# Two network blocks in one program: stage barriers replaced by stage counters, and five small reorderings

## The reference

```python
h = rmsnorm(x, norm_g[0]);  x = x + fox_mixer(h, ...)        # attention with a forget gate, 16 heads
h = rmsnorm(x, norm_g[1]);  x = x + nsa_mixer(h, ...)        # three attention branches, 16 heads
x = rmsnorm(x, final_g)
h = _rmsnorm(x, norm_mix[0]); x = x + _hgrn2_mixer(h, ...)   # gated recurrence, 8 heads of 128
h = _rmsnorm(x, norm_ffn[0]); x = x + _conv_ffn(h, ...)
h = _rmsnorm(x, norm_mix[1]); x = x + _mla_mixer(h, ...)     # latent attention, 8 heads
h = _rmsnorm(x, norm_ffn[1]); x = x + _conv_ffn(h, ...)

def _conv_ffn(h, w_up, conv_w, conv_b, w_down):              # 1024 -> 2 x 2816 -> 1024
    u = h @ w_up                                             # y: causal taps over 3 tokens of u, plus conv_b
    gate, up = jnp.split(y, 2, axis=-1)
    return (jax.nn.silu(gate) * up) @ w_down
```

## Time and profile before

| what | value |
|---|---|
| median of 3 runs | 1015.6 us (1015.43 to 1016.73) |
| time of the profiled execution | 1011.34 us |
| its span, first to last instruction | 1009.6 us |
| mean granted TensorE clock | 0.992 |
| PE, PE weight loads, DVE, ACT, POOL busy | 97%, 91%, 76%, 55%, 7% |
| bytes moved | 153.16 MB, mean 152 GB/s |

### The profile page before, as it was taken

The page is one execution under the profiler, slowest core; times in us unless marked ns, Lnnn a source line. Parts: engine busy times, 40 slices in busy tenths (PEclk is TensorE's granted clock), DMA queues, the critical chain, the costliest instruction groups (busy, mean ns, idle before and its releaser), DMA issues. The chain is left out here.

```text
span 1009.6 us, 19673 instructions
## 1 busy us (share of the span) xinstructions
PE 978.9 (97%) x7864; PEld 919.4 (91%) x7864; DVE 763.7 (76%) x1296; ACT 552.1 (55%) x873; POOL 66.8 (7%) x54
## 2 busy tenths in 40 slices
PE   7999999999999999999999999999999998999998
PEld 5999999898788999899999999999997898999996
DVE  5765776867887768498667888788868667788886
ACT  4644555365666656553566555555675464555552
POOL 3100004000000410000030000000001420000000
PEclk9999999999999999999999999999999998999999
DMA  9644445793212556500464767575531454766661
GB/s 279 178 128 131 130 146 154 219 298 110 84 43 83 156 180 187 190 1 1 148 187 134 210 198 208 167 212 164 153 125 43 125 153 139 206 180 200 192 184 42
DMA packets 184434, 153.16 MB, mean 152 GB/s; under 512 B 12509, under 2 KB 176932, under 8 KB 184356
## 3 DMA queue, kind: packets, MB, share of 16 engines
q1 hardware_dynamic: 184146, 152.01, 51.1%
q10 hardware_dynamic: 210, 0.05, 0.0%
HBM read 148.91 MB, written 1.05 MB: 149 GB/s over the span
## 5 line engine op out<-in xcount | busy, mean ns | idle before, releaser
L447 PE MATMUL bank<-h_high,w_high 128*128 128x256 f32 x1312 | 372.2, 284 | 4.8 <-DVE work L2013 1.5
L448 PE MATMUL bank<-h_low,w_high 128*128 128x256 f32 x1312 | 364.9, 278 | 0.0
L449 PE MATMUL bank<-h_high,w_low 128*128 128x256 f32 x1312 | 364.7, 278 | 0.0
L399 ACT ACTIVATE w_high<-ring 128x2048 fp32r<-128x2048 f32 x137 | 261.8, 1914 | 138.7 <-PE bank L449 131.4
L409 DVE TENSOR_TENSOR w_low<-ring,w_high 128x2048 fp32r<-128x2048 f32 x118 | 270.3, 2292 | 25.7 <-ACT w_high L399 25.2
L447 PEld LDWEIGHTS bank<-h_high,w_high 128*128 128x128 f32 x1312 | 248.2, 189 | 7.1 <-issue 5.4
L448 PEld LDWEIGHTS bank<-h_low,w_high 128*128 128x128 f32 x1312 | 248.3, 189 | 0.8 <-issue 0.5
L449 PEld LDWEIGHTS bank<-h_high,w_low 128*128 128x128 f32 x1312 | 248.1, 189 | 0.0
L1116 ACT ACTIVATE ffn_conv<-ffn_normed,par 128x256 f32<-128x256 f32 x88 | 48.1, 594 | 68.0 <-DVE ffn_normed L1129 67.9
L1138 DVE SCALAR_TENSOR_TENSOR ffn_conv<-ffn_normed,par,ffn_conv 128x254 f32<-128x254 f32 (+1 forms) x176 | 77.1, 480 | 7.4 <-ACT ffn_conv L1116 2.3
L795 ACT ACTIVATE work<-bank,work 128x128 f32<-128x128 f32 (+1 forms) x112 | 47.7, 432 | 47.5 <-DVE work L777 36.7
(11 more groups left out here) (359 smaller groups left out, 1873.4 us busy)
## 6 DMA issues: line engine op xcount, KB each, us to landing
ring<-in_ffn_w_up_dram SPq DMA_DIRECT2D x44, 1024.0 KB, 6.1
ring<-in_ffn_w_down_dram SPq DMA_DIRECT2D x22, 1024.0 KB, 5.2
ring<-in_fox_w_in_dram SPq DMA_DIRECT2D x16, 1024.0 KB, 6.0
ring<-in_hgrn_w_in_dram SPq DMA_DIRECT2D x16, 1024.0 KB, 5.5
ring<-in_nsa_w_in_dram SPq DMA_DIRECT2D x14, 1024.0 KB, 5.8
ring<-in_fox_w_out_dram SPq DMA_DIRECT2D x4, 1024.0 KB, 5.1
ring<-in_nsa_w_out_dram SPq DMA_DIRECT2D x4, 1024.0 KB, 5.2
ring<-in_hgrn_w_out_dram SPq DMA_DIRECT2D x4, 1024.0 KB, 5.4
```

What stands on the lines that cost most here:

```text
L399: i = nc.scalar.activation(dst, src, ACT.Copy)
L447: nc.tensor.matmul(o, ah, bh, start=start, stop=False, **kw)
L448: nc.tensor.matmul(o, ah, bl, start=False, stop=False, **kw)
L449: return nc.tensor.matmul(o, al, bh, start=False, stop=stop, **kw)
```

## The change

1. **One block.** All seven stages stand in one `nc.Block()`, so that no barrier stands between them. ACT, DVE and POOL drain at a stage's end and raise a counter. `entered(eng, stage)` at the head of each stage waits for the counters of the other engines and for a semaphore that PE raises anyway.
2. **NSA's memsets** of `kz2` wait on POOL for the spread row's copy (`n_row`).
3. **HGRN.** The exponents of head 0, second half of the tokens, are computed and exponentiated ahead of the last value tile; the two spreads stand two chunks later in their tile.
4. **FFN, start.** `normed` of pair 1 stands ahead of `multiply` of pair 0; the table of Silu is loaded right after the first two `high`. In FFN1 the first quarter of `x` is turned in the middle of pair 1, and quarters 0 and 1 are copied before and after the first `tap`. In FFN0 the four bf16 products of zeros go, and six fp32r products of zeros (128 x 512) stand between pair 1 and the loop.
5. **FFN, end.** `normed` and `tap` of pairs 20 and 21 stand in a row, ahead of the convolutions.
6. **Start.** `keep_warm` issues twice as many products of half the width.

The diff without the changes of indentation (the same `entered` and `drain` lines of the other engines and stages are left out):

```diff
-        zeros_bf = sb("zeros_bf", [P, 512], BF16)
+        zeros_bf, zeros_r = sb("zeros_bf", [P, S], BF16), sb("zeros_r", [P, P], F32R)
...
             for _ in range(n):
-                nc.tensor.matmul(B[5][:, :], zeros_bf[:, 0:P], zeros_bf[:, :], start=True, stop=True)
+                nc.tensor.matmul(B[5][:, 0:S], zeros_bf[:, 0:P], zeros_bf[:, :], start=True, stop=True)
+                nc.tensor.matmul(B[5][:, S:2 * S], zeros_bf[:, 0:P], zeros_bf[:, :], start=True, stop=True)
...
+                    if half and (e, c) == (0, DC - 1):
+                        half()
...
+            def copy_rows(act, q):
+                act.wait_ge(x_turned, 4 + q + 1)
+                nc.scalar.activation(x_rows[:, q // 2, q % 2 * 512:(q % 2 + 1) * 512], B[3 - q % 2][:, :],
+                                     ACT.Copy).then_inc(x_placed, 1)
...
-                ffn_pair(pe, pair_tile(1), u0 + 1, (u0 + 1) // 2, quarter=lambda: nrm.spread(pe))
-                turn_x(pe, 0)
+                ffn_pair(pe, pair_tile(1), u0 + 1, (u0 + 1) // 2, quarter=lambda: nrm.spread(pe),
+                         half=lambda: turn_x(pe, 0))
...
-                for b in range(4, 8):
-                    nc.tensor.matmul(B[b][:, :], zeros_bf[:, 0:P], zeros_bf[:, :], start=True, stop=False,
-                                     skip_group_check=True)
                 ffn_pair(pe, pair_tile(1), u0 + 1, (u0 + 1) // 2, quarter=lambda: nrm.spread(pe))
+                in_parts(pe, t0 + 2)
+                pe.wait_ge(bank_free[u0 % 2], u0 // 2 + 1)
+                for b in (4, 5, 4, 5, 6, 7):
+                    nc.tensor.matmul(B[b][:, :], zeros_r[:, :], h_hi[:, 0:2, :], start=True, stop=False,
+                                     skip_group_check=True)
...
                 high(act, t0 + 3)
+                nc.scalar.activation(scratch[:, :], eps[:, :], ACT.Silu)
+                if not following:
+                    copy_rows(act, 0)
                 for j in range(2):
                     tap(act, j)
+                    if not following and j == 0:
+                        copy_rows(act, 1)
                     high(act, t0 + 4 + j)
                     gate(act, j)
                 if not following:
...
+                    copy_rows(act, 2)
+                    copy_rows(act, 3)
...
-                for g in range(2):
-                    two_pairs(18 + 2 * g, 30 + 3 * g)
+                two_pairs(18, 30)
+                for j in (20, 21):
+                    tap(act, j)
+                for j in (20, 21):
+                    gate(act, j)
...
+        def entered(eng, stage):
+
+            if stage == 0:
+                return
+            if eng is not nc.scalar:
+                eng.wait_ge(act_over, stage)
+            if eng is not nc.vector:
+                eng.wait_ge(dve_over, stage)
+            if eng is not nc.gpsimd:
+                eng.wait_ge(pool_over, stage if stage < 5 else 4 if stage == 5 else 5)
+            if eng is not nc.tensor:
+                eng.wait_ge(*pe_over[stage])
...
+                act.drain().then_inc(act_over, 1)
...
+                pool.wait_ge(n_row, nrm_nsa.n + 1)
                 for b in range(2):
                     i = nc.gpsimd.memset(kz2[b], 0.0)
...
-                    by_feature(pe, t_f + i, hsp, between=lambda q, i=i: (i, q) == (1, 0) and nrm_hgrn.spread(pe))
+                    by_feature(pe, t_f + i, hsp, ready=lambda c, i=i: (i, c) == (1, 6) and nrm_hgrn.spread(pe))
...
+                for i in range(4):
+                    if i == 3:
+                        pe.wait_ge(lf_split, 4)
+                        pe.wait_ge(levels_in, 1)
+                        exponents(0, 1)
+                    by_token(pe, t_i + i, hsp)
...
                     if i == 3:
-                        nc.scalar.activation(scratch[:, :], eps[:, :], ACT.Exp)
+                        exps(0, 1)
```

More of the change, by code:

```diff
@@ L984, in build, with ffn_pair @@
         up_convolved = sem("ffn_up_convolved")
-        def ffn_pair(pe, t, u, bank_wait, ready=None, later=0, quarter=None):
+        def ffn_pair(pe, t, u, bank_wait, ready=None, later=0, quarter=None, half=None):
             in_parts(pe, t, later)
@@ L1349, in build @@
-        f0, fz = T["fox"], T["fox_z"]
-        fox_first = tile_first(f0, by_token)(nrm_fox)
-        fl, w_f_ready = sem("fox_f_loaded"), sem("fox_f_weights_ready")
-        with nc.Block() as block:
             @block.sync
             def _(sp):
+                entered(sp, 4 + 2 * l)
+                for t in range(sp_from, t0 + 5):
+                    load(sp, t)
+                with sp.Fori(0, NLOOP - 1) as i:
+                    for off in range(5, 11):
+                        load_ffn(sp, off, i)
@@ L1473, in steps_of @@
-        def steps_of(n, half):
-            return steps_at.get(2 * (n - 3) + half, ()) if n >= 3 else ()
-        with nc.Block() as block:
+                dve.drain().then_inc(dve_over, 1)
+            memory.open(less=2 * DC * S)
+            o_hi, o_lo = [memory.float32r("fox_out_" + n, DC, S) for n in ("high", "low")]
+            area = Area()
+            f_raw, f_abs, f_exp, f_log = [area(TT * FOX_H) for _ in range(4)]
+            logf = area(TT, FOX_H)
+            c_rest = area(2, TT, FOX_H)
@@ L1478, in _, with steps_of @@
+            def steps_of(n, half):
+                return steps_at.get(2 * (n - 3) + half, ()) if n >= 3 else ()
             @block.sync
             def _(sp):
+                entered(sp, 1)
                 n_late.append(load_params(sp, range(2, 6), loaded_p2))
@@ L1544, in _ @@
             def _(act):
+                entered(act, 1)
                 def evacuate(n):
@@ L1764, in steps_of @@
-        def steps_of(t, q):
-            return slot_steps.get(4 * (t - FIRST) + q, ())
-        with nc.Block() as block:
+                dve.drain().then_inc(dve_over, 1)
+            memory.open(less=CLEN * P)
+            b_hi, b_lo = [memory.float32r("blocks_" + n, CLEN // 2, P) for n in ("high", "low")]
+            o_hi, o_lo = [b[:, :, :].rearrange("p i n -> p (i n)").rearrange("p (c t) -> p c t", c=DC)
+                          for b in (b_hi, b_lo)]
+            area = Area()
+            raw_c = area(2, 2, S)
@@ new lines, in build @@
+            dec = area(2, 8, S)
+            late = area.same(2 * 8 * S)(12 * P)
+            sm = area(2, TT, 512)
+            fT = area.same(2 * TT * 512)(DC, S)
+            scx = area(2, P)
+            area(2, P)
+            lmask = area(512)
+            gT = area(DC, S)
+            oh = h
+            sq8 = keyT
+            roots = area(2 * HG_H)
+            t_f, t_q3, t_i, t_g = T["hgrn_f"], T["hgrn_q"], T["hgrn_i"], T["hgrn_g"]
+            for t in range(t_f + 1, t_g + 4):
+                plan_tile(t)
```

841 lines of the change are left out of this document (431 added, 410 removed).

## The result

The changed kernel takes 997.3 us (median of four runs, 997.18 to 997.46), the kernel before beside it 1015.6 (1015.43 to 1016.73): a ratio of 0.982 (95% interval 0.980 to 0.983), 18.3 us less. The two profiled executions, 1011.34 and 997.18 us, differ by only 14.2 us, where the sum had 14.55. So most of the error lies between the profiled execution of before and its median; how well the single steps held is taken up further down.

A forecast was written before the change was run, and what follows sets the result against it. PE, busy 978.9 of 1009.6 us, was taken as the bound, with gains only at stage heads and ends. Terms summed to -14.55 us: 996.8 against the profiled 1011.3, 1001.1 against the median 1015.6; range 997.0 to 1005.8.

The forecast's parts named there:

- the sum: Whole program: all terms added to -14.55 us, giving 996.8 against the profiled execution and 1001.1 against the median.
- FFN0's head: Start of FFN0: wait for `normed` of pair 1 goes (-0.8), products of zeros cost more (+0.45): -0.35 us.
- FFN1's head: Start of FFN1: PE's 4.1 us wait for ACT's copies and the half clock behind it go: -6.8 us.
- The ends: End of each FFN: PE's wait for the last `hidden` goes, 1.6 us each, -3.2 in all.
- The barriers: Six stage ends: counters let PE's sequencer pass ahead of the array, so idle pauses go: -3.3 us.
- NSA's head: Start of NSA: memsets held back, spread row ready sooner, PE's 0.5 us wait for `low` goes: -0.65 us.
- HGRN's exponents: HGRN, last value tile: moving the exponents buys nothing, since PE's idle time changes place: +0.45 us.
- The clock at HGRN's head: Start of HGRN: half of the 1.4 us lost to the slow clock returns as barrier idle goes: -0.7 us.
- the three terms of HGRN: HGRN: its share of the barriers (0.65 us gained), the exponents (+0.45) and the clock at its head (-0.7).
- rivals: Five alternative outcomes: four faster than before (chances 0.12, 0.12, 0.07, 0.08), one slower, FFN groups becoming DVE's (0.03).
- DVE doesn't hold FFN1 back: Denies a rival: in FFN1 PE waits for DVE's splits, some 4 of 6.8 us return, 1005; chance 0.12.
- the halves of `keep_warm` and the later spreads in HGRN: Program start and HGRN: `keep_warm` runs while input is on its way, later spreads follow needed work: no cost.

The follow-up runs named there:

- after_old_copies: The changed kernel with FFN1's transposes and copies of x put back as before: 1003.2 us (6 runs).
- before_zeros: The kernel before with six fp32r products of zeros at FFN0's loop entry instead of four bf16 at the stage's start, and halved `keep_warm` products: 1010.7 us.
- after_bf16_zeros: The changed kernel with its six products of zeros ahead of FFN0's loop in bf16 instead of fp32r: 998.1 us (6 runs).
- best_four_zeros: The changed kernel with HGRN's exponents as before and four products of zeros ahead of FFN0's loop instead of six: 996.8 us.
- after_pause: The changed kernel with one more PE wait ahead of pair 3, in the first turn of FFN0's loop only: 998.6 us against 996.1.
- after_old_head0: The changed kernel with FFN0's head as before (four bf16 products of zeros, pair 1 scaled behind all of pair 0): 1001.9 us (6 runs).
- before_copies: The kernel before with only the change's order at FFN1's head (transposes, copies, early table load): 1008.3 us against 1015.6.
- before_again: The kernel before, unedited, run again: twelve runs, six from 1006.3 to 1011.0 us and six from 1014.9 to 1016.7; profiled at 1015.9.
- before_ends: The kernel before with only the change's order at both FFN ends (normed and tap of pairs 20 and 21 in a row): 1012.1 us, 3.5 less.
- best_hgrn_zeros: best_four_zeros with two more fp32r products of zeros of 512 columns in HGRN, behind the tile where the roots are spread: 996.1 us.

## Why the prediction was wrong

**The step that failed** is the last of the sum: "against the median of 1015.6, which lies 4.3 above it, 1001.1". I carried the 4.3 us unchanged, as if they belonged to the launch or to profiling. They belonged to FFN0: the profiled execution had the quick rhythm there (188.7 us), and those of the median, by their times, the slow one (194.5 us in the profile of such a run). All 16 runs of the unchanged changed kernel lie at 995.0 to 1000.1, with no group 6 us apart. With it fell the term **FFN0's head: -0.35 us**. Putting the old head back cost 6.1. I had priced the pause (0.63 and 0.15) and the zeros (0.45), and not what stands behind the pause: some 1400 products at 4.3 ns more each, some 6 us (5.7 by the two stages' lengths). With 5.7 more the sum against the median would have been -20.3, or 995.3, two below what came; against the profile it held as it was, since that execution had the quick rhythm.

That it held to 0.4 us (14.2 for 14.55) is in part luck. For the start, FOX, NSA, HGRN, FFN0, MLA and FFN1 the two profiles differ by -1.7, -0.5, +0.7, -0.1, -3.1, -0.2 and -9.4 us; the terms had 0, -0.65, -1.1, -0.9, -2.5, -0.3 and -9.05. The start is shorter by a fall of the clock at 16.5 us that came in one execution and not in the other, and NSA is longer by the one near 226 us.

The other steps, one by one:
- **FFN1's head, -6.8:** 6.8 by the stage's length with this part alone. Without the half clock behind it 4.1 (after_old_copies), the lower bound.
- **The ends, -1.6 each:** 1.7 and 1.8.
- **The barriers, -3.3:** 2.3 to 3.8 by the medians, with the 1.4 of the clock at HGRN's head in it, so 0.9 to 2.4 without; the waits come to 3.0 us, and the pause at FFN1 to 0.61 for 0.65. The term is the right kind and probably too large.
- **NSA's head, -0.65:** the wait of 0.8 us that returns. The `low` beside the memsets was unharmed, as the Trainium skill's rule ("SBUF — State Buffer", Who interferes with whom) has it.
- **HGRN's exponents, +0.45:** right in sign and in mechanism, probably too small: 0.8 to 1.5 by the stage in profiles with the quick rhythm, 0.8 by medians that the noise does not separate.
- **The clock at HGRN's head, -0.7:** the whole 1.4. These last two errors cancel: from before to four profiles of variants with the change in HGRN and the quick rhythm the stage falls from 175.2 to 174.3 us, the 0.9 that the three terms of HGRN gave. In the profile of the changed kernel itself it is 175.0, only 0.1 less, since PE there ran the stage's first part in the slow rhythm (rows below: 281 products for 294 in 33 us).
- Of the **rivals**, none came true: DVE doesn't hold FFN1 back, and PE is busy for all 114.00 us from 836 to 950.
- Not tried apart: the halves of `keep_warm` and the later spreads in HGRN, priced at nothing.

HGRN's first part in before, then in the changed kernel, columns as in the earlier trace rows:

```profile
362.00:395.00 33.00, 33.00 (x294) 33.00 (x293) 28.34 (x38) 21.48 (x17) 2.52 (x1) 1.00 0.57 175
```

```profile
362.00:395.00 33.00, 33.00 (x281) 33.00 (x281) 26.45 (x36) 19.51 (x16) 1.09 (x1) 1.00 0.63 195
```

**What stays open.** That FFN0's head decides how many runs have the slow rhythm in its loop is shown both ways, by the runs' times and the profiles: the old head brings it into the changed kernel, and the six products of zeros take it out of the kernel before. How the head does it is not shown. The slow rhythm was seen to start at interruptions of PE, and never in the loop where the margin at the first down product was about 1 us or more (no upper group among the 16 runs of the changed kernel and 6 each of before_zeros, after_bf16_zeros, best_four_zeros and after_pause; one run of after_old_copies, 1007.5, is in doubt). But whether a given pause brings it is not settled: 0.1 us did in all of after_old_head0's runs, by their times, but not in the profile of before_copies; 0.7 us did in none of after_pause's, and 0.63 us in 6 of 12 of before_again's; and in before_ends it was there ahead of the pause. Nor is it shown what in PE differs between the two. No run took the wait at pair 3 away by other data or changed the order of PE's waits there.

## What to carry to other kernels

Before a sum is set against a median, ask whether the profiled execution is one of the median's kind: compare its time with the single runs, and where they differ, find the stage that can hold the difference before predicting. In a long row of products without waits, compare products per stretch between two profiles of the same kernel, not only waits and clock. And give the first waits of such a loop a margin of a microsecond or more: that is cheap, and in these profiles no kernel that had it fell into the slow rhythm there, which cost some 50 times the pause of 0.1 us in after_old_head0. Whether the margin is the cause is not shown.

## What the runs showed of the hardware

- PE has two rhythms for the same row of fp32r products of 256 columns, at a granted clock of 1.00 and with no wait: 113 and 117 to 118 ns from start to start. Either lasts until PE is interrupted or turns to products of another kind, here up to 173 us (before_again). Two products of 512 columns in between didn't change it (best_hgrn_zeros). The slow one also stands in HGRN's first part in some profiles, the changed kernel's among them (281 products for 294 in 33 us).
- Runs of one kernel thereby fall into groups: of the runs of the kernel before, none lies between 1012.1 and 1013.3 us, and the share above differed between the sets of runs, from 23 of 29 and 11 of 11 to 4 of 11 and 2 of 10 (beside one of 3448 us, left out and not explained), so that its median was 1015.8 in one and 1010.6 in another.
- At HGRN's head a barrier, with half a microsecond of idle time behind sixteen one-column products, went with a fall to 1.2 GHz over 3.4 us in all seven profiles that had it, and in none of the thirteen without.
